# Forming the bonus product as the last of a pair's operands in a fused RWKV-7 and attention kernel

## The reference, cut to what matters

```python
kk = heads(k * k_k)
kk = kk / jnp.maximum(jnp.sqrt(jnp.sum(jnp.square(kk), axis=-1, keepdims=True)), 1e-12)
k = k * (1.0 + (a - 1.0) * k_a)
...
y = delta_rule_scan(r_h, heads(decay), k_h, v_h, -kk, kk * a_h)
...
bonus = (jnp.sum(r_h * k_h * r_k, axis=-1, keepdims=True) * v_h).reshape(B, T, MIX_WIDTH)
return (y + bonus) * g, q_mem
```

## Time and profile before

| | before |
|---|---|
| median of 3 runs | 1566.65 us (1565.47 to 1569.39) |
| the profiled execution's own time | 1561.43 us |
| its span, first to last instruction | 1559.6 us |
| TensorE (PE) busy | 1475.0 us, 95% |
| VectorE (DVE) busy | 821.7 us, 53% |
| ScalarE (ACT) busy | 549.8 us, 35% |
| POOL busy | 238.1 us, 15% |
| mean granted TensorE clock | 0.989 of full speed |

### The profile page before, as it was taken

The page is one execution under the profiler, slowest core; times in us unless marked ns, Lnnn a source line. Parts: engine busy times, 40 slices in busy tenths (PEclk is TensorE's granted clock), DMA queues, the critical chain, the costliest instruction groups (busy, mean ns, idle before and its releaser), DMA issues.

```text
span 1559.6 us, 26654 instructions
## 1 busy us (share of the span) xinstructions
PE 1475.0 (95%) x11374; PEld 1163.7 (75%) x11374; DVE 821.7 (53%) x1267; ACT 549.8 (35%) x937; POOL 238.1 (15%) x166
## 2 busy tenths in 40 slices
PE   6898889887799999999999999999999999999999
PEld 4676666665588888888878776766777888888887
DVE  3656666676446354444564348678564443444343
ACT  4544234335332222221352236565334231222121
POOL 0123222320110000000020002222312220220120
PEclk9899999999999999999999999999999999999999
DMA  8120100020023323232222233221222323232223
GB/s 314 42 82 30 43 29 30 30 83 3 29 95 95 99 91 105 84 108 83 93 95 82 83 107 95 89 75 55 68 94 82 99 92 107 88 101 95 95 85 105
DMA packets 39333, 130.88 MB, mean 84 GB/s; under 512 B 4272, under 2 KB 5296, under 8 KB 39216
## 3 DMA queue, kind: packets, MB, share of 16 engines
q1 hardware_dynamic: 39216, 129.18, 25.7%
HBM read 127.07 MB, written 2.10 MB: 83 GB/s over the span
## 4 chain that ended last, share of the span: by engine, by line
PE 79%; DVE 10%; ACT 5%; issue 3%; DMA 1%; POOL 0%; SPq 0%; POOLq 0%; DVEq 0%; ACTq 0%
PE bank L1007 77%; PE bank L1406 1%; ACT Whi L2045 1%; DMA x<-in_xT 1%; DVE Wlo L1602 1%; DVE qa L1713 1%; DVE Xi L1845 1%; DVE kf L1755 1%; DVE z L1639 0%; DVE ftmp L1659 0%; DVE qa L1711 0%; DVE slab L1733 0%; PE bank L1120 0%; PE bank L1196 0%; DVE X L1684 0%
## 5 line engine op out<-in xcount | busy, mean ns | idle before, releaser
L1007 PE MATMUL bank<-Hhi,Whi 128*128 128x512 f32 x912 | 378.3, 415 | 18.7 <-DVE Wlo L1602 12.9
L1007 PE MATMUL bank<-Hhi,Wlo 128*128 128x512 f32 x912 | 363.6, 399 | 0.0
L1007 PE MATMUL bank<-Hlo,Whi 128*128 128x512 f32 x912 | 360.4, 395 | 0.0
L1007 PE MATMUL bank<-Uhi,Whi 128*128 128x512 f32 x736 | 291.6, 396 | 13.6 <-DVE Wlo L1602 7.9
L1007 PE MATMUL bank<-Uhi,Wlo 128*128 128x512 f32 x736 | 287.6, 391 | 0.0
L1007 PE MATMUL bank<-Ulo,Whi 128*128 128x512 f32 x736 | 287.4, 391 | 0.0
L2045 ACT CAST Whi<-Wraw 128x1024 fp32r<-128x1024 f32 (+1 forms) x216 | 223.0, 1036 | 161.3 <-PE bank L1007 149.8
L1602 DVE TENSOR_TENSOR Wlo<-Wraw,Whi 128x1024 fp32r<-128x1024 f32 (+1 forms) x175 | 223.9, 1281 | 100.6 <-ACT Whi L2045 100.5
L1007 PEld LDWEIGHTS bank<-Hhi,Whi 128*128 128x128 f32 x912 | 173.6, 190 | 74.8 <-DVE Wlo L1602 14.9
L1007 PEld LDWEIGHTS bank<-Hlo,Whi 128*128 128x128 f32 x912 | 173.7, 190 | 42.8
L1007 PEld LDWEIGHTS bank<-Hhi,Wlo 128*128 128x128 f32 x912 | 174.1, 191 | 33.3
(11 more groups left out here) (293 smaller groups left out, 1591.8 us busy)
## 6 DMA issues: line engine op xcount, KB each, us to landing
Wraw<-in_wts SPq DMA_DIRECT2D x208, 512.0 KB, 3.5
bA<-in_biasA SPq DMA_DIRECT2D x12, 256.0 KB, 2.7
Wraw<-in_wts SPq DMA_DIRECT2D x8, 384.0 KB, 3.0
x<-in_xT SPq DMA_DIRECT2D x8, 256.0 KB, 4.8
x_rows<-in_xN SPq DMA_DIRECT2D x2, 1024.0 KB, 8.3
X<-in_xT SPq DMA_DIRECT2D x2, 1024.0 KB, 7.9
out<-X SPq DMA_DIRECT2D x8, 256.0 KB, 2.1
bB<-in_biasB SPq DMA_DIRECT2D x4, 384.0 KB, 3.0
```

The source lines that it names most:

```text
L1007: return e.matmul(o, lhsT, rhs, start=start, stop=stop, skip_group_check=True)
```

## The change

On VectorE the product `tm` moves out of `key_rows` into a function of its own, `bonus_rows`, which `operands` calls last. `operands` gets a wait for `kn`, which `key_rows` made before itself. ScalarE's copy into the next pair's r slab now waits for `rk` and no more for `AR[.., 1]`, since `tm` is now the last to read r. No other engine's program changes.

```diff
         def key_rows(p):
-            tm = ftmp_of(("sq", p))
             b = MB[plan.M.at["kk", p]]
             w.wait_ge(S["kk"], p + 1)
             w.wait_ge(S["bt"], 2 * p)
             e.scalar_tensor_tensor(kn[:], k_[:], v("kk", p), b[:], ALU.mult,
                                    ALU.mult).then_inc(S["spread_out"])
+
+        def bonus_rows(p):
+
+            tm = ftmp_of(("sq", p))
             w.wait_ge(S["bt"], 2 * p + 1)
             w.wait_ge(S["spread_out"], N("spread", "kk", p))
             e.scalar_tensor_tensor(tm[:], r_[:], v("rk", p), kf[:], ALU.mult, ALU.mult).then_inc(S["rk"])
...
         def operands(p):
             w.wait_ge(S["exp"], 2 * p + 1)
+            w.wait_ge(S["spread_out"], N("spread", "kk", p))
             if p >= 2:
                 w.wait_ge(S["yo2"], p - 1)
...
             e.tensor_tensor(stk(ar[:, 1, :]), stk(r_), Pp[:, :, 1:65], ALU.mult).then_inc(S["ar"])
+            bonus_rows(p)
...
                     p = x.key[0] - 1
                     if x.key[1] == 0:
-                        w.wait_ge(S["ar"], 2 * p + 2)
+                        w.wait_ge(S["rk"], p + 1)
                     elif x.key[1] == 1:
```

## The result

| | before | after |
|---|---|---|
| median | 1566.06 us (1562.52 to 1569.39, 4 executions) | 1548.22 us (1547.42 to 1550.27, 4 executions) |
| ratio after/before | | 0.9888, 95% interval 0.9867 to 0.9908 |
| the profiled execution, its span | 1561.43, 1559.6 us | 1548.16, 1546.4 us |
| mean granted TensorE clock | 0.989 | 0.991 |

The change makes the kernel 17.8 us faster, 1.1%. The forecast was 11.4 us and the range ended at 1551, so the direction is right and the size is outside. (A fourth execution of the kernel before, 1562.52, moved its median from 1566.65 to 1566.06.) A second set of executions of the changed kernel gave 1548.79 (1547.87 to 1550.31), ratio 0.9885 with interval 0.9859 to 0.9911.

What follows compares the result with a forecast made beforehand. TensorE, busy 95% of the span, was taken as the bound. Stalls gave 7.5 + 0.5 + 0.3 = 8.3 us, with the clock 11.4, so the median 1566.65 would become 1555.2; range 1551 to 1562.

Steps and rivals of the forecast that it cites:

- the place where it goes away: Pairs 2 to 5: without the product in front, `Xi` starts 1.88 us earlier, TensorE's stall goes from 2.56 to 0.68; gain 7.5.
- the new place is covered: Pairs 2 to 5: behind the last operand the product takes about 0.68 us, within VectorE's idle time before `Yi`, costing nothing.
- what is late next: Pairs 2 to 5: after the change TensorE still waits for `Xi`, behind `kn`, for 0.68 us, not for its own work.
- the sum's first value: Pair 1: `T` comes 0.7 us earlier if POOL's product keeps to 1.26, 0.4 with 1.55; 0.5 was taken.
- Rival C: `Xi` is held by POOL until 225.32, or another wait replaces the stall: 1.9 us gained, no clock gain, 1564.8; chance 0.13.
- rivals B and E: B: stalls shrink, clock doesn't follow, 1558.3, chance 0.29. E: new slow stretches behind other stalls, 1572 and more, chance 0.03.
- Pair 2 repeats pair 3, pair 5 repeats pair 4: TensorE's clock in pairs 2 to 5: two slow stretches of 1.58 us each follow the stalls; 3.1 taken as won.
- The 5.2: Whole kernel: the median, 1566.65 us, lay 5.2 above the profiled execution; the same 11.4 was subtracted from it, giving 1555.2.
- rival D: Timed runs have slow stretches in all four pairs, 2 to 5, and all go: -14.5 us, 1552.2; chance 0.07.
- at most 0.55 can be won: Pair 0: `qm` starts at 65.94, TensorE's last matmul for it ends at 65.39; 0.3 us taken, bounds 0 and 0.55.

Runs made afterwards that it cites:

- pair 0 alone: The kernel before with the product moved in pair 0 only, the other pairs as before: 1564.86 us against 1567.64, ratio 0.9985.
- the product formed twice: The changed kernel with the product formed a second time in pairs 2 to 5, in its old place directly behind `kn`: 1559.24 us.

## Why the prediction was right or wrong

All five profiled executions of the kernel before and both of the changed one give this account, in us:

| part of the span | forecast | before, mean of 5 | after, mean of 2 | gain |
|---|---|---|---|---|
| first instruction to `kn` of pair 0 | 0 | 63.8 | 63.5 | 0.3 |
| to `xm` of pair 0 | 0.3 | 24.5 | 22.0 | 2.5 |
| to `xm` of pair 1 | 0.5 | 39.1 | 38.4 | 0.7 |
| to `xm` of pair 5, without slow clock: stalls | 7.5 | 207.8 | 200.3 | 7.5 |
| the same, slow clock | 3.1 | 6.2 | 0 | 6.2 |
| to the end | 0 | 1221.7 | 1222.4 | -0.7 |
| sum | 11.4 | 1563.1 | 1546.7 | 16.4 |

The medians differ by 17.8. The other 1.4 is no part of these spans: the five profiled executions of the kernel before took 1564.9 on average, the median of the four timed ones was 1566.06.

**Right:** the place where it goes away (1.88 forecast, 1.89 measured, four times), its cause (held beside POOL: 1.03 by the run in which POOL waits), that `Xi` isn't held there, that the new place is covered (0.74 each, no new wait), what is late next (still `Xi`, 0.67), and that the slow stretches behind these stalls go. Pair 1 was 0.7, the sum's first value, where I took 0.5; `kn` to `T` fell from 6.50 to 5.81. (In pair 1 the old product was held beside POOL's `Wlo L2362`, 118.62 to 121.00, and not beside `ta`, which started at 121.15.) Rival C is refuted by the 48 `Xi L1850` above, rivals B and E by the clock of 1.00 in this piece.

**Wrong, the step that failed:** "Pair 2 repeats pair 3, pair 5 repeats pair 4: two slow stretches, 3.1 within 0.1", and "I subtract the same 11.4" from a median that lay 5.2 over the profiled execution. The reading was right for that execution: its two slow stretches stand in pairs 2 and 3. But the term was sized on one execution, which turned out to be the one with the least slow clock of five: the five hold 3.1 to 8.9, mean 6.2, and the changed kernel none. The bound was short as well: it allowed one slow stretch for each of the four stalls, 6.2 in all, but two executions had 8.8 and 8.9, since slow stretches also stood behind the waits for `PD`, in pairs that had the long stall as well, and in one of the two executions two stood in a row behind a long stall, twice. The 5.2 "for reasons that no view shows" was in the main the same thing: executions of the kernel before at 1565.92 to 1568.38 show a mean clock of 0.985 or 0.986, the profiled one 0.989, and the changed kernel's ten 0.991 or 0.992. I had written this down as rival D, with 0.07, and its 14.5 is 3.3 short too: 2.2 of that is pair 0.

**The second, smaller miss:** pair 0, 0.3 forecast, 2.5 measured. "TensorE's last matmul for it ended at 64.99+0.40 = 65.39, so at most 0.55 can be won" took a matmul as the limit of `qm` that `qm` doesn't need: in the run with the product behind `Xi`, `qm` started 1.49 before the same work of TensorE ended (64.43 against 65.92). In all six moved executions `qm` started 1.05 or 1.06 after `kn`, against 2.95 to 2.98. Part of the 2.5 is again a slow stretch, present in 5 of 7 executions and in none of 6 (1.54 without it), for which the forecast had no term in pair 0.

The Trainium skill, page "TensorE: Matmul & The Clock Gate", Part 1, on the HAM clock gate, says that the monitor runs on its own time, so that one kernel shows another number of slow matmuls in another run. The runs agree in that: five executions of one kernel show 2 to 6 slow stretches in the same piece of work.

Before the result, the size of this was in view only as the gap between one execution and the median.

What brings a slow stretch is shown in part. The piece of pairs 2 to 5 was profiled in seven executions with four stalls of 2.56: the five of the kernel before with 3.1 to 8.9 us of slow clock, pair 0 alone with 7.3 (215.1 long, five slow stretches), the product formed twice with 1.6. In these seven, a slow stretch begins at 18 of the 28 long stalls, and at 7 of the 28 waits of 1.50 for `PD`; each of those seven is followed by another at the long stall 17 us later. In the five executions with stalls of 0.67 or none, it begins at none of the stalls and at 1 of the 20 waits for `PD`; with stalls of 1.52 at none of four, and at 1 of the 4 waits for `PD`. So a stall of 2.56 is where most of them begin, but it is neither enough nor needed, and 7 of 28 against 1 of 20 is too few to say that the long stalls also bring those at `PD`. That the long stalls cost clock is shown by taking them away: four executions at 1.00 and one at 0.99, where seven had 0.95 to 0.99. Putting them back alone brought back only part of it (2.9 in the median, against 6.2 in the mean of the five). What decides for one execution and not for the next was not tried.

## What to carry to other kernels

An instruction that nobody waits for can still be the longest stall of the bound engine, if it stands in front of one that is waited for, and more so if another engine's traffic stretches it (1.78 here instead of 0.75): read the queue behind it, not who waits for it. Before a gain is sized from one profiled execution, set it beside the median of the others. A gap between the two that no view explains is a term of the sum, and where stalls of the bound engine bring its clock down, as here, a change that removes them can win more than their length, and most of the scatter with it.

## What the runs showed of the hardware

- TensorE at the same work in the same kernel, no other engine's busy time changed, took 210.9 to 216.7 us for one piece at mean clocks from 0.98 to 0.95. The executions of the kernel with four stalls of 2.56 us spread over 16 us, the ten of the kernel with 0.67 over 3. Mean clock and time went together: 1558.07 to 1565.08 at 0.988 or more, 1565.92 to 1574.03 at 0.986 or less, in the 57 executions of the kernel before that were run beside the others.
- A slow stretch of TensorE, about 3.4 us at the lower level, began at 18 of 28 stalls of 2.56 us, at 0 of 16 stalls of 0.67, and at 9 of 52 waits of 1.50, in 13 profiled executions of eight kernels.
- A VectorE product of two SBUF tensors (128x512) took 0.74 to 0.75 with POOL idle. It took 1.31 when it started 0.51 after POOL's product, 1.54 at 0.30 after (pair 1 with the product behind `Xi`) and 1.78 at 0.02 after: it ends 0.54 to 0.56 after POOL in each case. A 128x256 addition with one operand in PSUM took 0.41 to 0.43 in all 48 cases, beside POOL or not.
